# Gate and up projections by seven block products for eight, high parts first

## The reference

```
h = x + concat(pool_mixer(u), attention(q, k, v)) @ w_out      # u, q, k, v = rms_norm(x) @ w_in
hn = rms_norm(h)
y = h + (silu(hn @ w_gate) * (hn @ w_up)) @ w_down
```

## Time and profile before

| | |
|---|---|
| time, median of 3 runs | 2284.66 us |
| the profiled execution's own time | 2285.82 us |
| its span | 2284.0 us |
| PE busy | 2227.1 us (98%) |
| DVE busy | 868.4 us (38%) |
| ACT busy | 701.7 us (31%) |
| POOL busy | 609.5 us (27%) |
| mean DMA share, bytes | 195.50 MB, mean 86 GB/s |

### The profile page before, as it was taken

How to read it: one execution, slowest core, us unless ns; L and a number is a source line. 1 busy time by engine, 2 the same in 40 slices (tenths; PEclk the granted TensorE clock), 3 DMA queues, 4 the chain that set the end, 5 groups by cost and what they waited for, 6 DMA issues and landing times.

```text
span 2284.0 us, 32102 instructions
## 1 busy us (share of the span) xinstructions
PE 2227.1 (98%) x13246; PEld 2030.9 (89%) x13246; DVE 868.4 (38%) x1500; ACT 701.7 (31%) x1756; POOL 609.5 (27%) x282
## 2 busy tenths in 40 slices
PE   6999999988999899999999999999999999999999
PEld 6888888866878899999999999999999999999997
DVE  5565565561111233332332333233333233233334
ACT  5666666542333221121212121122212121212111
POOL 1000000061442224232433233232423232232321
PEclk9999999989999999999999999999999999999999
DMA  6011111035654431222222531222122422222121
GB/s 174 27 40 47 38 38 33 20 116 161 213 173 132 129 125 56 74 74 65 66 74 65 166 125 58 72 74 71 59 74 74 161 71 73 64 66 74 56 74 69
DMA packets 233498, 195.50 MB, mean 86 GB/s; under 512 B 20605, under 2 KB 209834, under 8 KB 233354
## 3 DMA queue, kind: packets, MB, share of 16 engines
q1 hardware_dynamic: 230954, 184.80, 25.8%
q10 hardware_dynamic: 2400, 8.65, 1.0%
HBM read 158.50 MB, written 35.03 MB: 85 GB/s over the span
## 4 chain that ended last, share of the span: by engine, by line
PE 91%; DMA 2%; ACT 2%; SPq 2%; DVE 2%; POOL 1%; issue 1%; ACTq 0%
PE ps L639 27%; PE ps L641 27%; PE ps L640 27%; PE ps L735 2%; PE ps L709 2%; PE ps L823 1%; PE ps L721 1%; SPq L368 1%; PE ps L653 1%; DMA xt_lo_raw<-mix_d 1%; PE ps L825 1%; PE ps L821 1%; PE ps L697 1%; DMA w_lo_raw<-in_w_gate 1%; ACT s_sb L972 1%
## 5 line engine op out<-in xcount | busy, mean ns | idle before, releaser
L573 POOL TENSOR_TENSOR w_lo<-w_lo_raw,w_hi 128x1024 fp32r<-128x1024 f32 x198 | 470.7, 2405 | 1042.3 <-ACT w_hi L1038 521.8
L639 PE MATMUL ps<-xb_hi,w_hi 128*128 128x352 f32 x2112 | 686.6, 325 | 7.0 <-POOL w_lo L573 4.1
L641 PE MATMUL ps<-xb_lo,w_hi 128*128 128x352 f32 x2112 | 684.7, 324 | 0.0
L640 PE MATMUL ps<-xb_hi,w_lo 128*128 128x352 f32 x2112 | 683.8, 324 | 0.0
L639 PEld LDWEIGHTS ps<-xb_hi,w_hi 128*128 128x128 f32 x2112 | 398.0, 188 | 8.8 <-issue 7.4
L640 PEld LDWEIGHTS ps<-xb_hi,w_lo 128*128 128x128 f32 x2112 | 400.0, 189 | 1.2
L641 PEld LDWEIGHTS ps<-xb_lo,w_hi 128*128 128x128 f32 x2112 | 397.5, 188 | 0.0
L1059 ACT ACTIVATE sg<-ps 128x352 f32<-128x352 f32 x132 | 61.2, 464 | 1061.0 <-PE ps L641 1060.9
L1275 DVE TENSOR_TENSOR aa<-ps,sg 128x352 f32<-128x352 f32 x132 | 69.2, 525 | 817.6 <-PE ps L641 789.5
L1294 DVE TENSOR_TENSOR h<-ps,h 128x512 f32<-128x512 f32 (+1 forms) x396 | 273.0, 689 | 189.8 <-PE ps L641 187.5
L641 PE MATMUL ps<-w_lo,act_hi 128*128 128x512 f32 x660 | 257.1, 390 | 0.0
(11 more groups left out here) (102 smaller groups left out, 2295.2 us busy)
## 6 DMA issues: line engine op xcount, KB each, us to landing
w_lo_raw<-in_w_gate SPq DMA_DIRECT2D x66, 512.0 KB, 3.7
w_lo_raw<-in_w_up SPq DMA_DIRECT2D x66, 512.0 KB, 3.8
w_lo_raw<-in_w_down SPq DMA_DIRECT2D x66, 512.0 KB, 4.3
xb_lo_raw<-hn_d SPq DMA_DIRECT2D x3, 2816.0 KB, 10.6
xload<-in_x_prompt SPq DMA_DIRECT2D x16, 512.0 KB, 4.4
mix_d<-o_st SPq DMA_DIRECT2D x64, 128.0 KB, 1.8
xt_lo_raw<-mix_d SPq DMA_DIRECT2D x16, 512.0 KB, 6.2
wg_hi_raw<-in_x_prompt SPq DMA_DIRECT2D x16, 512.0 KB, 6.7
```

Source lines behind the costliest of these rows:

```text
L573: nc.gpsimd.tensor_tensor(lo, raw, hi.bitcast(F32), ALU.subtract).then_inc(done, 1)
L639: nc.tensor.matmul(out, s_hi, m_hi, start=first, stop=False)
L640: nc.tensor.matmul(out, s_lo, m_hi, start=False, stop=False)
L641: return nc.tensor.matmul(out, s_hi, m_lo, start=False, stop=final)
```

## The change

Each step's gate and up are now two sets of products (`SETS`, 66 in all: set 2G is gate, set 2G + 1 is up, each 256 hidden columns by 704 tokens). A set is seen as a 2 x 2 by 2 x 2 block product (hidden halves by halves of the inner dimension, and these by token halves), and done by seven block products (`product(s, m)`, Strassen's scheme in Winograd's form) where the units before make eight: 7 x 12 matmuls of 128 x 352 for 8 x 12. In a product the four high by high matmuls come first, then a wait for the low weights, then the four low by high, then the four high by low. The sums that the scheme needs are new work:

- weights: 4 sums of 128 x 512 in a set on DVE (`weight_sum`), and 7 high (ACT, `high2`) and 7 low parts (POOL, `low2`) of 128 x 512 for 4 blocks of 128 x 512 before. The seven high parts have one buffer each for all sets;
- tokens: 4 sums of 128 x 1408 in a part (`rows_sum`, DVE), 7 high parts (ACT), 7 low parts (4 on DVE, 3 on POOL). They have one buffer for all parts, so the new part is made while the last `down` of the old one runs, which is put before the new part's first set;
- results: four banks of PSUM hold the products in turn; ACT copies the first product (`save_p1`), DVE makes two partial sums (`q7_sum`, `u2_sum`) and three results (`result_sum`). Products 3 to 6 each wait for one of these.

The activations now have one buffer, `w_down` has one pair of slots, the load order of SP is new, and `store_y` moves from ACT's queue to SP's. PE's order in a step is `products(2G)`, `down(G - 1)`, `products(2G + 1)`. The core of the diff:

```
+SETS = 2 * NG
+PRODUCTS = 7
+BANK_OF = (0, 1, 2, 0, 2, 1, 2)
+A_BLOCK = {0: (0, 0), 3: (0, 1), 5: (1, 1)}
+HALF_K = KT // 2
+RESULTS = ((0, 0), (1, 1), (1, 0), (0, 1))
+X_HIGHS = (0, 1, 4, 2, 3, 5, 6)
+X_LOWS_DVE = (0, 2, 4, 6)
+X_LOWS_POOL = (1, 3, 5)
...
+            xs_hi = sb("xs_hi", [PART, PRODUCTS, HALF_K, NB], F32R, scope=ffn)
+            xs_raw, xs_lo = twin("xs_lo", [PART, PRODUCTS, HALF_K, NB], ffn)
+            w2_hi = sb("w2_hi", [PART, PRODUCTS, HALF_K * PART], F32R, scope=ffn)
+            ws_raw, ws_lo = twin("ws_lo", [PART, 5, HALF_K * PART], ffn)
+            odd = twin("w2_lo1", [PART, 2, 2, HALF_K * PART], ffn)
+            even = twin("w2_lo0", [PART, 2, 2, HALF_K * PART], ffn)
...
+        def low_of(s, m):
+            if m in A_BLOCK:
+                i, j = A_BLOCK[m]
+                return w2_lo[s % 2][:, i, j]
+            return ws_lo[:, {1: 0, 2: 1, 4: 2, 6: 3 + s % 2}[m]]
...
+            def load_second_halves(p):
+                rows_stored(p)
+                if p > 1:
+                    sp.wait_ge(x_sum, 4 * p)
+                    sp.wait_ge(xs_split_dve, 4 * p)
+                load(b12[:, :, :], rows_block(p, 0, 1), b12_loaded)
+                load(b22[:, :, :], rows_block(p, 1, 1), b22_loaded)
+            def load_first_halves(p):
+                sp.wait_ge(product_done, after_product(last_set(p), 0))
+                load(xs_raw[:, 0], rows_block(p, 0, 0), b11_loaded)
+                sp.wait_ge(product_done, after_product(last_set(p), 3))
+                load(xs_raw[:, 3], rows_block(p, 1, 0), b21_loaded)
...
+            def load_gate_up(s):
+                if s == 0:
+                    sp.wait_ge(xn_ready, NTILES)
+                elif s == 1:
+                    sp.wait_ge(out_ready, 2 * NTILES)
+                else:
+                    sp.wait_ge(product_done, after_product(s - 2, 5))
+                a = 256 * (s // 2 % GROUPS)
+                for i in range(2):
+                    load(w2_raw[s % 2][:, i].rearrange("p j (k m) -> p (j k) m", k=HALF_K),
+                         (w_gate_k, w_up_k)[s % 2][:, :, a + PART * i:a + PART * (i + 1)], w2_loaded[s % 2])
...
             for G in range(NG):
                 p, j = divmod(G, GROUPS)
-                for n in range(4 if G + 1 < NG else 2):
-                    load_gate_up(G + 1, n)
+                if G > 0:
+                    load_gate_up(2 * G + 1)
+                    if j == 0:
+                        store_y(p - 1)
+                    load_down(G)
+                    if j == 0:
+                        for i in range(PT_TILES):
+                            load_h(p, i)
                 if j == 1 and p + 1 < PARTS:
-                    load_xb(p + 1)
-                if j == 0 and p > 0:
-                    for i in range(PT_TILES):
-                        load_h(p, i)
-                if 1 <= G < NG - 1:
-                    load_down(G)
+                    load_second_halves(p + 1)
+                if j == GROUPS - 1 and p + 1 < PARTS:
+                    load_first_halves(p + 1)
+                if G + 1 < NG:
+                    load_gate_up(2 * G + 2)
+            store_y(PARTS - 1)
...
+            def low2(s, m):
+                need(pool, w_sum, 4 * s + min(m + 1, 3))
+                low(w2_high, PRODUCTS * s + m + 1, low_of(s, m), raw_of(s, m), w2_hi[:, m], w2_split)
...
+            for s in range(SETS):
+                G, which = divmod(s, 2)
                 p, j = divmod(G, GROUPS)
+                for m in range(PRODUCTS):
+                    if s + 1 < SETS:
+                        low2(s + 1, m)
+                    if m == 2 and which == 1:
+                        low1(G)
+                if which == 1 and j == GROUPS - 1 and p + 1 < PARTS:
+                    for m in X_LOWS_POOL:
+                        rows_low(p + 1, m)
...
+            def product(s, m):
+                p, first = s // (2 * GROUPS), s % (2 * GROUPS) == 0
+                pe.wait_ge(w2_high, PRODUCTS * s + m + 1)
+                if first:
+                    pe.wait_ge(xs_high, PRODUCTS * p + X_HIGHS.index(m) + 1)
+                if m == 0:
+                    need(pe, c12_read, s - 1)
+                elif m == 1:
+                    need(pe, c11_read, s)
+                elif m == 2:
+                    need(pe, c21_read, s)
+                else:
+                    pe.wait_ge((p1_saved, u2_ready, q7_ready, c22_read)[m - 3], s + 1)
+                out, hi, lo = product_bank(s, m), w2_hi[:, m], low_of(s, m)
+                cols = [slice(PART * k, PART * (k + 1)) for k in range(HALF_K)]
+                for k in range(HALF_K):
+                    nc.tensor.matmul(out, hi[:, cols[k]], xs_hi[:, m, k], start=m < 3 and k == 0, stop=False,
+                                     skip_group_check=True)
+                pe.wait_ge(w2_split, PRODUCTS * s + m + 1)
+                for k in range(HALF_K):
+                    nc.tensor.matmul(out, lo[:, cols[k]], xs_hi[:, m, k], start=False, stop=False, skip_group_check=True)
+                if first:
+                    if m in X_LOWS_DVE:
+                        pe.wait_ge(xs_split_dve, 4 * p + X_LOWS_DVE.index(m) + 1)
+                    else:
+                        pe.wait_ge(xs_split_pool, 3 * p + X_LOWS_POOL.index(m) + 1)
+                for k in range(HALF_K):
+                    last = nc.tensor.matmul(out, hi[:, cols[k]], xs_lo[:, m, k], start=False, stop=k == HALF_K - 1,
+                                            skip_group_check=True)
+                last.then_inc(product_done, 1)
+            def products(s):
+                for m in range(PRODUCTS):
+                    product(s, m)
...
+                if G % GROUPS == 0:
+                    down(G - 1)
+                products(2 * G)
+                if G % GROUPS > 0:
+                    down(G - 1)
+                products(2 * G + 1)
             down(NG - 1)
         @block.scalar
...
+            def high2(s, m):
+                if s == 0:
+                    act.wait_ge(wo_free, 1)
+                else:
+                    act.wait_ge(product_done, after_product(s - 1, m))
+                if m in A_BLOCK:
+                    act.wait_ge(w2_loaded[s % 2], 32 * (s // 2 + 1))
+                else:
+                    act.wait_ge(w_sum, 4 * s + {1: 1, 2: 2, 6: 3, 4: 4}[m])
+                nc.scalar.activation(w2_hi[:, m], raw_of(s, m), ACT.Copy).then_inc(w2_high, 1)
             def high1(G):
...
+            def save_p1(s):
+                act.wait_ge(product_done, after_product(s, 0))
+                need(act, c12_read, s - 1)
+                nc.scalar.activation(p1[:, s % 2, :], product_bank(s, 0), ACT.Copy).then_inc(p1_saved, 1)
...
+                save_p1(s)
+                for m in range(3):
+                    if s + 1 < SETS:
+                        high2(s + 1, m)
+                if which == 1:
+                    high1(G)
+                if s == 1:
+                    act.wait_ge(hn_stored[1], 16 * (NTILES // 2))
+                for n in range(4):
+                    if s == 0 and n < 2:
+                        stage_copy(NTILES - 1, n)
+                    if which == 0:
+                        gate(G, n)
+                    else:
+                        high_part(G, n)
+                    if s + 1 < SETS:
+                        high2(s + 1, n + 3)
...
+            def weight_sum(s, n):
+                m = (1, 2, 6, 4)[n]
+                if n == 0:
+                    dve.wait_ge(w2_loaded[s % 2], 32 * (s // 2 + 1))
+                else:
+                    dve.wait_ge(w_sum, 4 * s + n)
+                if s == 0:
+                    dve.wait_ge(wo_free, 1 if n == 0 else 2)
+                elif n != 2:
+                    dve.wait_ge(product_done, after_product(s - 1, m))
+                raw = w2_raw[s % 2]
+                a, b, op = ((raw[:, 0, 0], raw[:, 1, 0], ALU.subtract),
+                            (raw[:, 1, 1], raw_of(s, 1), ALU.subtract),
+                            (raw[:, 0, 1], raw_of(s, 2), ALU.subtract),
+                            (raw[:, 1, 0], raw[:, 1, 1], ALU.add))[n]
+                nc.vector.tensor_tensor(raw_of(s, m), a, b, op).then_inc(w_sum, 1)
...
+            def activations(s):
+                G, p, more = s // 2, s // (2 * GROUPS) + 1, s + 1 < SETS
+                new_part = more and (s + 1) % (2 * GROUPS) == 0
+                q7_sum(s)
+                if more:
+                    weight_sum(s + 1, 0)
+                u2_sum(s)
+                if more:
+                    weight_sum(s + 1, 1)
+                    weight_sum(s + 1, 2)
+                act_product(G, 0)
+                if new_part:
+                    rows_sum(p, 0)
+                result_sum(s, 1)
+                if s == 1:
+                    for b in range(3):
+                        dve.wait_ge(h_stored[b], 16 * len(range(b, NTILES, 3)))
+                    for b in range(2):
```

(83 more changed lines are left out.)

319 lines of the change are left out of this document (175 added, 144 removed).

## The result

The changed kernel takes 2505.5 us in the median (2498.1 to 2510.7, four runs) where the kernel before takes 2284.9: a ratio of 1.0957, 95% interval 1.0921 to 1.0992, 9.6% slower. The forecast was 2489 us. The profiled execution has a span of 2496.3 us, against 2488.5 of the sum.

What follows compares the result with a forecast made beforehand. Prediction took PE's matmul count to bound the kernel before. Sum: 2284.0 - 128.1 - 8 + 30x8.9 + 2x4.3 + 2x31 + 3 = 2488.5; forecast 2489 us, 8-in-10 range 2240 to 2560.

Steps and rivals of the forecast that it cites:

- Removed, 128.1 us: Gate and up on PE: 24 of 192 matmuls fewer per step at 161.8 ns, 3.88 us, times 33 steps.
- The load: Even sets' weights, queued behind w_down's, land at about t = 8.5; product 4 of odd sets stalls 2.1 us.
- The lock: DVE operations with both inputs in SBUF wait for the running POOL operation to end; 17 such per step for 6.
- The schedule: Each pair of sets: PE stalls of 2.1, 1.4, 3.9 and 1.0 us at products 4, 2, 3 and 4.
- the 8.9 us: Loss per pair of sets: four stalls summing to 8.4 us plus 0.5 us of slow clock.
- the rival that was slower by less: Two of four stalls vanish: 4 to 6.6 us in a step, 2300 to 2386 us; chance 13%.
- Part ends, 31 us each: Two part ends: product 4 stalls 9 us, down waits some 12, then some 7 within it, 1 for the clock.
- `load_second_halves`, 4.3 us: In two steps these token loads go ahead of the weights: 1.4 MB, 4.3 us each.
- Start, -8 us: Kernel start: before loses 2.9 + 4.1 us and 4 to the clock; the new start waits some 3 us.
- the cheap lock: DVE mostly finds POOL idle, leaving the load's 2.1 us and 10 us per part end: 2247 us; chance 19%.
- all is hidden: Loads land early as well and all added work hides beside PE: 2158 us; chance 6%.
- The rival of another distance: The new matmul order changes the distance by some 5 ns, 28 us over 5544 gate and up matmuls; chance 2%.

Runs made afterwards that it cites:

- the last kernels: Changed kernel with loads early, sums on POOL, low1 last, save_p1 and u2_sum early: 2192.7 us; the same with part ends reordered: 2186.2 us.
- four more moves: Against the changed kernel, besides loads early: low1 with high1 last, weight sums on POOL, save_p1 early, u2_sum early; 2192.7 us, ratio 0.9588.
- the second reordered kernel: The kernel before, eight products in eight, with only its gate and up matmuls reordered, high parts first: 2287.1 us, ratio 0.9999.

## Why the prediction was right

Step by step, after's span against the sum of 2488.5:

- **Removed, 128.1 us.** Right in count; mis-sized in the distance. The earlier trace rows gave 161.8 ns, and the products of after that neither wait nor run slowly take 1.90 us or 1.94, that is 158.3 or 161.7 ns. At 158.3 a step saves 4.5 us instead of 3.9.
- **The load.** Issue at t = 1.0, landing at 8.5, `weight_sum` 0 ahead of `u2_sum`, product 4 at 9.8: each as forecast. Undone alone, the odd set's stall is gone.
- **The lock.** `weight_sum` means 1.51 and 1.12 us where 0.69 is the time alone, `act_product` 1.24; the long rows end just behind POOL's, and with narrow POOL operations the even sets' wait is gone.
- **The schedule.** Predicted 2.1, 1.4, 3.9 and 1.0 us of stall and 0.5 of slow clock; sets 35 and 36 show 2.0, none, 3.3 and none, the mean of the 24 pairs 3.0, 0.3, 3.3 and none. The 1.4 us at product 2 rarely shows (L1481: 8.6 us in 7 waits) because the clock stretched the odd set before it; with the load early, when the odd set is short, it is there in 30 sets. So the term that was mis-sized most is the clock, 0.5 us in a pair. I took 2.1 us of idle to fall between 1.78 with the clock at 1.00 and 2.25 with 0.51, and let it cost nothing. Behind 2.02 us it was 0.59. Products 4 and 5 of odd sets are together 1.6 us over their 1.90 each, and products 3 and 4 of even sets 1.4: 3 us in a pair. So the 8.9 us were right by luck: stalls of 6.6 us for 8.4, slow clock 3 for 0.5. The sets themselves are shorter (42.0 us without a gap for 42.6), and a step of 51.9, 9.9 us over them, came out for 51.5. Two of the four stalls all but vanished, as the rival that was slower by less had it, but not its 2300 to 2386 us, because the clock took that time back.
- **Part ends, 31 us each.** Measured 28: product 4 waits 9.3 us (predicted 9), `down` 11.0 (12), and is 5.2 longer (7); the set takes 36.56 us. `load_second_halves`, 4.3 us: that set is 4.5 longer than the mean in one part (22.46), 5.6 in the other (23.55).
- **Start, -8 us.** Mis-sized by 7. I had 3 us lost in the new start for 11 in the old. Before lost 12.2 up to the end of its first `down` (77.6 took 89.8). In after, the first gate and up matmul comes at 734.8 (before 731.0), and set 0 takes 20.7 us, 7.1 over the 13.6 of the sum: 10.9 lost. Its wait for set 1's load is 3.5 us (some 3 forecast); what I left out is the slow clock beside it, and the later first matmul. The latter need not be the change's: the kernel before with only its matmuls reordered has it at 735.4. Sets 1 and 2 are a pair like the others, 8.6 us over.
- **The total.** It misses by no more than 8 because errors cancel. Against the sum's 161.8 ns the 30 pairs lose 284.6 us where it had 275.6 with the two loads of tokens, 9 more; the start is 7 more, the two part ends 6 less, the end 2 less.

Part end, the rows of DVE in after with the load that sets it:

```profile
1290.41 0.69 DVE L1433 TENSOR_TENSOR ws_lo_raw<-w_lo_raw 128x512 f32<-128x512 f32 x1 [11.29 <-DMA w_lo_raw<-in_w_gate]
...
1303.26 2.69 DVE L1453 TENSOR_TENSOR xs_lo_raw<-b,xs_lo_raw 128x1408 f32<-128x1408 f32 x1
```

Of the rivals, the cheap lock (2247) fell with the even sets' wait; that all is hidden needed the load early and four more moves; in the regular steps the last kernels make it true. The rival of another distance has its answer in the second reordered kernel: none from the order.

## What to carry to other kernels

Work that moves from the full engine to idle ones pays only if their in-order queues can take it: read, for each result that the full engine waits for, what stands ahead of it in its producer's queue and what load that waits on. Issue such loads first, keep long POOL operations away from DVE operations with two SBUF inputs that a result stands behind, and mend all links of a late chain together, since one alone only moves the wait. Seven products for eight cost 9.6% as first ordered and give 4.1% after five moves.

## What the runs showed of the hardware

- **What one hold costs.** A DVE operation with two SBUF inputs ends just behind the POOL operation that it meets, 0.1 us (64 columns), 0.4 (352) and 0.55 (512) later: 2.19 us for 64 columns, 2.71 for 352, 2.89 for 512, against 0.21, 0.51 and 0.69 alone. One with an input in PSUM is not held (0.51 to 0.53 throughout). GPSIMD Engine Reference (the Trainium skill, Key points) names contention for the first kind; the traces agree, and the price is the POOL operation's remaining time, so two of 2.4 us cost much and those of 32 columns (0.25 us) next to nothing (`weight_sum` 0.69 us in the mean).
- **POOL is slowed as well**: 1.29 us for 512 columns when alone, 1.5 to 1.6 and more beside DVE. In after POOL's operation of 1673.14 meets a `weight_sum` begun 0.04 us earlier, which keeps its 0.69 us, and takes 1.79 itself: the one that began first is not held. A POOL sum of two raw blocks takes the same 1.3 us as a subtraction.
- **A short idle time can cost the clock.** Behind 2.0 us idle the next 3 us had 0.59; elsewhere 1.78 us left it at 1.00, and so did the 1.5 us ahead of product 3 in the kernel with the sums on POOL. In after the two stalls of a pair so bring about 1.5 us more each.
- **The distance of equal matmuls is not constant**: 161.7 ns in both kernels with eight products, 158.3 in most sets of those with seven, all at a granted clock of 1.00. In after both occur in one step: behind `down` mostly 158.3, from a step's first stall on mostly 161.7. Nothing here explains it.
- **Landing by place in the queue**: the gate loads take 7.0 us in the median behind w_down's pair, 5.1 when issued first.
